# Weighted expert rows added onto the residual rows by indirect DMA, in a streaming encoder step on one Trainium2 core

## The reference

```python
h   = LN0(x) * (1 + scale_m(c)) + shift_m(c)
mix = W_out [ RetentionGroup(h) | StickBreakingGroup(h) ]   # one combined input projection
x   = LN_m(alpha * x + gate_m(c) * mix)                     # x1 below
h   = LN0(x) * (1 + scale_f(c)) + shift_f(c)                # h2 below
x   = LN_f(alpha * x + gate_f(c) * HierMoE(h))
```

## Time and profile before

| what | value |
|---|---|
| median of three runs (lowest, highest) | 1428.81 us (1427.43, 1430.86) |
| the profiled execution's own time | 1431.01 us |
| its span | 1428.9 us |
| PE busy, of the span | 1288.4 us (90%) |
| DVE, ACT, POOL busy | 800.3, 591.2, 335.2 us (56%, 41%, 23%) |
| mean granted clock of TensorE | 0.962 |
| DMA, mean over the span | 164 GB/s |

### The profile page before, as it was taken

One profiled execution on the slowest core, in us unless ns is written; L12 is line 12 of the kernel. 1 busy time (PEld: TensorE's weight loads), 2 busy tenths in 40 slices (PEclk: granted clock), 3 DMA queues, 4 the chain that ended last, 5 costly groups with the idle time before them and its releaser, 6 DMA issues.

```text
span 1428.9 us, 19774 instructions
## 1 busy us (share of the span) xinstructions
PE 1288.4 (90%) x7219; PEld 996.1 (70%) x7220; DVE 800.3 (56%) x1042; ACT 591.2 (41%) x781; POOL 335.2 (23%) x449
## 2 busy tenths in 40 slices
PE   3899999999999989999999988999999999999800
PEld 1665778887787656656687877887777888887700
DVE  5634232324502166666699974557888242558678
ACT  0423022322212267677612232456777253457432
POOL 0032320002200166676346520000000000000073
PEclk9899999999999999999999999999999999999955
DMA  9746110102121261211423378667999161649773
GB/s 337 294 163 196 58 67 1 60 0 75 44 60 42 66 182 31 52 40 31 148 89 104 111 281 352 236 226 278 384 391 389 64 235 59 235 168 381 265 253 121
DMA packets 138776, 234.54 MB, mean 164 GB/s; under 512 B 57328, under 2 KB 58936, under 8 KB 138712
## 3 DMA queue, kind: packets, MB, share of 16 engines
q1 hardware_dynamic: 128440, 196.41, 39.2%
q0 software_dynamic: 6496, 23.60, 4.8%
q10 hardware_dynamic: 3776, 13.67, 2.3%
HBM read 197.96 MB, written 35.68 MB: 164 GB/s over the span
## 4 chain that ended last, share of the span: by engine, by line
PE 63%; issue 12%; DVE 9%; ACT 5%; POOL 5%; DMA 4%; SPq 1%; ACTq 1%; POOLq 0%; DVEq 0%
PE psum L826 58%; POOL arena L2076 3%; PE psum L1051 2%; ACT high L1495 2%; DMA arena<-in_w_ada_ffn 2%; PE psum L1236 1%; DMA arena<-in_w_ada_mix 1%; DVE arena L2015 1%; DVE arena L2014 1%; DVE arena L2007 1%; DVE arena L2005 1%; DVE arena L2006 1%; ACT a_high L1527 1%; PE psum L1242 1%; DMA arena<-h_rows,smalls 1%
## 5 line engine op out<-in xcount | busy, mean ns | idle before, releaser
L826 PE MATMUL psum<-win_high,x_low 128*128 128x512 f32 (+1 forms) x432 | 169.9, 393 | 0.0
L826 PE MATMUL psum<-high,h_high 128*128 128x512 f32 x416 | 164.5, 395 | 2.5 <-DVE h_low L1961 2.5
L826 PE MATMUL psum<-win_high,x_high 128*128 128x512 f32 (+1 forms) x416 | 166.3, 400 | 0.0
L826 PE MATMUL psum<-high,h_low 128*128 128x512 f32 x416 | 162.8, 391 | 0.0
L826 PE MATMUL psum<-win_low,x_high 128*128 128x512 f32 (+1 forms) x416 | 162.8, 391 | 0.0
L826 PE MATMUL psum<-arena 128*64 128x128 f32 (+9 forms) x1324 | 139.4, 368 | 22.1 <-DMA arena<-in_w_ada_mix 17.4
L826 PEld LDWEIGHTS psum<-arena 128*64 128x64 f32 (+6 forms) x1324 | 70.5, 142 | 73.7 <-issue 45.7
L1809 DVE TENSOR_TENSOR_SCAN arena<-arena,psum 128x512 f32<-128x512 f32 (+4 forms) x116 | 109.5, 978 | 19.4 <-ACT arena L1452 19.2
L1956 DVE TENSOR_TENSOR low_odd<-raw_odd,high 128x2048 fp32r<-128x2048 f32 x48 | 107.8, 2288 | 13.7 <-ACT high L1495 13.7
L1956 DVE TENSOR_TENSOR low_even<-raw_even,high 128x2048 fp32r<-128x2048 f32 x48 | 107.7, 2287 | 10.9 <-ACT high L1495 10.8
L2076 POOL TENSOR_TENSOR arena<-arena 128x512 f32<-128x512 f32 (+4 forms) x116 | 108.2, 932 | 9.3
(11 more groups left out here) (264 smaller groups left out, 2475.5 us busy)
## 6 DMA issues: line engine op xcount, KB each, us to landing
raw_even<-in_w_e_gate SPq DMA_DIRECT2D x8, 2048.0 KB, 10.6
raw_even<-in_w_e_up SPq DMA_DIRECT2D x8, 2048.0 KB, 16.5
raw_even<-in_w_e_down SPq DMA_DIRECT2D x8, 2048.0 KB, 14.6
raw_odd<-in_w_e_gate SPq DMA_DIRECT2D x8, 2048.0 KB, 10.4
raw_odd<-in_w_e_up SPq DMA_DIRECT2D x8, 2048.0 KB, 16.7
raw_odd<-in_w_e_down SPq DMA_DIRECT2D x8, 2048.0 KB, 14.8
win<-in_w_in SPq DMA_DIRECT2D x7, 2048.0 KB, 7.9
expert_rows<-arena ACTq DMA_DIRECT2D x26, 512.0 KB, 6.3
```

What stands on the lines that cost most here:

```text
L826: pe_last[0] = nc.tensor.matmul(*x, **y)
```

## The change

- The tensor `expert_rows` is gone. The DRAM tensor of the x1 rows has 128 rows more and that of the h2 rows one more, for slots without a row; SP fills them early with two small DMAs.
- Routing scales w0 and w1 by 1/alpha and splits them into three bf16 parts (six DVE operations on 128x18 or half of that). POOL multiplies the table of slots with each part (three products of 128x594), PE makes 54 small products (128x33) behind the first block's turn, and ACT copies the result, `slot_w`: for every slot its weight, in one column set for prompt rows and another for stream rows. Two more DVE operations make `si`, the row that a slot's result is added to.
- In a block, ACT makes `gate_rows` as the second gate times the slot's weight in place of the copy and the store. DVE adds the first gate times its weight to that (128x1024, from SBUF) and multiplies the down product in PSUM with it into `yb`. These two stand behind pieces 1, 2, 3 of the next weights and ahead of pieces 4, 5. POOL adds `yb` onto the x1 rows in DRAM by an indirect DMA with an add, issued behind the gather for a later block. The product into `yb` waits until the addition before has landed.
- ACT waits for `rows8` ahead of the first block. SP loads expert 1 only when the first gather has landed, and `rows8` behind expert 1. The zero fill is gone.
- In the tail SP loads the nine tiles of summed rows in four groups, once the last addition has landed. DVE takes mean and variance of tiles 0 and 1 by itself; for the others ACT takes the sum and the squares. Then power, norm and store as before.
- In the front `keep_clock` has 15 and 4 products instead of 8 and 5, and 6 new ones stand ahead of the first projection. The first weight chunk is split ahead of the rows, and the four turns of the cached keys of the first pair of heads stand two steps later.

```diff
@@ -375,7 +376,7 @@
-                cache_at[per_pair * pair + 2 + 2 * n] = (pair, n)
+                cache_at[per_pair * pair + 2 + 2 * n + 2 * (pair == 0)] = (pair, n)
@@ -441,8 +442,9 @@
         events.append(("h_turn", 0))
+        split_event("w", 0, 0)
         split_event("x", 0, None)
-        for c in range(KC):
+        for c in range(1, KC):
             split_event("w", 0, c)
@@ -779,18 +787,15 @@
             load_expert(0, 0, (1, 2))
+            sp.wait_ge(s_hg, 16)
             load_expert(1, 1)
-            sp.wait_ge(s_hg, 16)
+            sp.wait_ge(s_ids, 2)
             for slot, src in enumerate((mod_row(1, 0, 2), mod_row(1, 1, 2),
                                         ln_ffn_g[0].unsqueeze(0).to_broadcast([P, D]),
                                         ln_ffn_b[0].unsqueeze(0).to_broadcast([P, D]))):
                 sp.dma_start(rows8[:, slot, :], src).then_inc(s_router, 16)
-            sp.wait_ge(s_zero, 1)
-            total = sp.value_load(table[0:1, 16:17], min_val=1, max_val=MAX_BLOCKS - 1)
-            with sp.Fori(total, MAX_BLOCKS) as b:
-                sp.dma_start(y_dram[bass.ds(b * P, P), :], zero_rows).then_inc(s_fill, 16)
@@ -801,10 +806,11 @@
-            sp.wait_ge(s_edone, EXPERTS - 1)
-            for t in range(TILES):
-                r = rows_of(t)
-                sp.dma_start(x1c[t][0:r], x1_dram[t * P:t * P + r, :]).then_inc(s_x1i, 16)
+            sp.wait_ge(s_summed, 1)
+            for i, tiles in enumerate(SUM_GROUPS):
+                for t in tiles:
+                    r = rows_of(t)
+                    sp.dma_start(ya[t][0:r], x1_dram[t * P:t * P + r, :]).then_inc(s_sum_in[i], 16)
@@ -840,7 +846,7 @@
                     if j >= 2:
-                        keep_clock((8, 5)[j - 2], 4)
+                        keep_clock((15, 4)[j - 2], 4)
@@ -975,6 +981,7 @@
                     if ev[1] == 1:
+                        keep_clock(6, 0)
                         proj(0)
@@ -1217,7 +1224,17 @@
             pe.wait_ge(s_route, 1)
+            pe.wait_ge(s_gi, 2)
             block_turn(0)
+            for s in range(2):
+                tiles = [n for n in range(18) if (n % 9 == LAST) == bool(s)]
+                for part in range(3):
+                    pe.wait_ge(s_bw, part + 1)
+                    for n in tiles:
+                        r = rows_of(n % 9)
+                        last = mm(bank(6)[:, s * MAX_BLOCKS:(s + 1) * MAX_BLOCKS], place_oh[0:r, n, :], block_w[0:r, part, n, :],
+                                  start=(part == 0 and n == tiles[0]), stop=(part == 2 and n == tiles[-1]))
+            last.then_inc(s_ids, 1)
@@ -1236,6 +1253,7 @@
+                        pe.wait_ge(s_gi, 3)
@@ -1505,8 +1523,13 @@
+            act.wait_ge(s_ids, 2)
+            act.wait_ge(s_gi, 2)
+            A(slot_w.rearrange("p s b -> p (s b)"), bank(6)[:, 0:2 * MAX_BLOCKS], ACT.Copy).then_inc(s_gi, 1)
+            act.wait_ge(s_gi, 3)
             act.sem_inc(s_ye, 1)
-            act.sem_inc(s_ys, 16)
+            act.wait_ge(s_ys, 16)
+            act.wait_ge(s_router, 128)
@@ -1531,11 +1554,9 @@
+                        act.wait_ge(s_ye, b + 1)
+                        A(gate_rows, rows8[:, 1], ACT.Copy, scale=slot_w[:, 1, bass.ds(b, 1)]).then_inc(s_gsA, 1)
                         act.wait_ge(s_yp, b + 1)
-                        act.wait_ge(s_ys, 16 * b + 16)
-                        A(yb.rearrange("p (a c) -> p a c", a=2), psum[2][:], ACT.Copy).then_inc(s_ye, 1)
-                        act.wait_ge(s_ye, b + 2)
-                        act.dma_start(y_dram[bass.ds(b * P, P), :], yb).then_inc(s_ys, 16)
...
@@ -1544,15 +1565,17 @@
+                    A(yc[t][0:r], ya[t][0:r], ACT.Copy, accum_out=fin_nm[0:r, t:t + 1]).then_inc(s_crs, 1)
...
@@ -1916,6 +1939,12 @@
             step(TT(w1, w0, dd, ALU.mult))
+            w18 = w01.rearrange("p a t -> p (a t)")
+            step(TS(w18, w18, 1.0 / ALPHA, None, ALU.mult))
+            for part in range(3):
+                step(V.tensor_copy(w_part[part], w18 if part == 0 else w_rest))
+                if part < 2:
+                    step(TT(w_rest, w18 if part == 0 else w_rest, w_part[part], ALU.subtract))
...
@@ -1944,9 +1973,10 @@
+            done(TS(gi, bank(2)[:, 0:MAX_BLOCKS], float(TOK), None, ALU.add), s_gi, 1)
+            step(TS(own_pad, bank(2)[:, 0:MAX_BLOCKS], 0.0, tok_f[:, 0:1], ALU.is_equal, ALU.mult))
+            done(STT(si[:, 1:MAX_BLOCKS + 1], bank(2)[:, 0:MAX_BLOCKS], float(TOK), own_pad, ALU.add, ALU.add), s_gi, 2)
@@ -1987,6 +2017,12 @@
+                        dve.wait_ge(s_gsA, b + 1)
+                        STT(gate_rows, rows8[:, 0], slot_w[:, 0, bass.ds(b, 1)], gate_rows, ALU.mult, ALU.add).then_inc(s_gsD, 1)
+                        dve.wait_ge(s_gsD, b + 1)
+                        dve.wait_ge(s_yp, b + 1)
+                        dve.wait_ge(s_ys, 16 * b + 32)
+                        TT(yb, psum[2].rearrange("p a c -> p (a c)"), gate_rows, ALU.mult).then_inc(s_ye, 1)
@@ -1995,24 +2031,22 @@
-                if t < TILES:
-                    r = rows_of(t)
-                    x = ya[t][0:r]
-                    dve.wait_ge(s_crs, t + 1)
-                    step(STT(x, yc[t][0:r], w1[0:r, t:t + 1], x, ALU.mult, ALU.add))
-                    step(TT(x, x, rows8[0:r, int(t == LAST)], ALU.mult))
-                    done(STT(x, x1c[t][0:r], ALPHA, x, ALU.mult, ALU.add, accum_out=fin_nm[0:r, t:t + 1]), s_cacc, t + 1)
-                    done(TS(fin_nm[0:r, t:t + 1], fin_nm[0:r, t:t + 1], -1.0 / D, None, ALU.mult), s_cve, t + 1)
...
+            for v in range(2):
+                dve.wait_ge(s_sum_in[v], 16 * len(SUM_GROUPS[v]))
+                for hh in range(2):
+                    step(V.bn_stats(stats[:, hh, :], ya[v][:, hh * 512:(hh + 1) * 512]))
+                step(V.bn_aggr(ln_mv[:, v, :], stats.rearrange("p a b -> p (a b)")))
+                step(TS(fin_nm[:, v:v + 1], ln_mv[:, v, 0:1], -1.0, None, ALU.mult))
+                done(TS(fin_sq[:, v:v + 1], ln_mv[:, v, 1:2], EPS / ALPHA ** 2, None, ALU.add), s_fve, v + 1)
+            for v in range(TILES):
+                r = rows_of(v)
+                if v >= 2:
+                    dve.wait_ge(s_csq, v - 1)
+                    done(TS(fin_sq[0:r, v:v + 1], fin_sq[0:r, v:v + 1], 1.0 / D, EPS / ALPHA ** 2, ALU.mult, ALU.add), s_fve, v + 1)
+                dve.wait_ge(s_cnm, v + 1)
+                x = ya[v][0:r]
+                done(STT(x, x, fin_nm[0:r, v:v + 1], rows8[0:r, 2], ALU.add, ALU.mult), s_cg, v + 1)
+                STT(x, x, ln_rstd[0:r, v:v + 1], rows8[0:r, 3], ALU.mult, ALU.add).then_inc(s_cy, 1)
@@ -2124,41 +2157,54 @@
+            pool.wait_ge(s_pad, 32)
+            pool.wait_ge(s_x1o[0], 80)
+            pool.wait_ge(s_x1o[1], 64)
+            pool.wait_ge(s_gi, 1)
+            pool.indirect_dma_start(hg, None, h2_dram, bass.IndirectOffsetOnAxis(ap=gi[:, 0:1], axis=0)).then_inc(s_hg, 16)
+            for part in range(3):
+                w_of_token = w_part[part].unsqueeze(2).to_broadcast([P, 18, MAX_BLOCKS])
+                G.tensor_tensor(block_w[:, part], block_oh, w_of_token, ALU.mult).then_inc(s_bw, 1)
+            pool.wait_ge(s_whg, 16)
             pool.wait_ge(s_gi, 2)
-            pool.indirect_dma_start(hg, None, h2_dram, bass.IndirectOffsetOnAxis(ap=gi[:, 0:1], axis=0)).then_inc(s_hg, 16)
+            pool.indirect_dma_start(x1_dram, bass.IndirectOffsetOnAxis(ap=si[:, 0:1], axis=0), gate_rows, None,
+                                    compute_op=ALU.add).then_inc(s_ys, 16)
+            pool.wait_ge(s_ids, 2)
+            step(G.memset(yb, 0.0))
...
                 pool.sem_inc(s_go, 1)
                 pool.indirect_dma_start(hg, None, h2_dram, bass.IndirectOffsetOnAxis(ap=idc[:, 0:1], axis=0)).then_inc(s_hg, 16)
-            pool.wait_ge(s_fill, 16 * MAX_BLOCKS)
+                pool.wait_ge(s_ys, 16 * b)
+                G.tensor_copy(idc[:, 1:2], si[:, bass.ds(b - 1, 1)]).then_inc(s_idx, 1)
+                pool.wait_ge(s_idx, 2 * b)
+                pool.wait_ge(s_ye, b)
+                pool.sem_inc(s_go, 1)
+                pool.indirect_dma_start(x1_dram, bass.IndirectOffsetOnAxis(ap=idc[:, 1:2], axis=0), yb, None,
+                                        compute_op=ALU.add).then_inc(s_ys, 16)
             pool.wait_ge(s_ys, 16 * total + 16)
+            pool.wait_ge(s_ye, total + 1)
             pool.sem_inc(s_go, 1)
+            pool.indirect_dma_start(x1_dram, bass.IndirectOffsetOnAxis(ap=idc[:, 1:2], axis=0), yb, None,
+                                    compute_op=ALU.add).then_inc(s_ys, 16)
+            pool.wait_ge(s_ys, 16 * total + 32)
             pool.wait_ge(s_edone, EXPERTS)
...
-                    pool.indirect_dma_start(dst[0:r], None, y_dram,
-                                            bass.IndirectOffsetOnAxis(ap=slot_i[0:r, kk, t:t + 1], axis=0)).then_inc(s_y0[t % 4], 16)
...
+            pool.sem_inc(s_summed, 1)
```

(52 more changed lines are left out.)

54 lines of the change are left out of this document (19 added, 35 removed).

## The result

The changed kernel takes 1436.83 us (five runs, 1436.36 to 1438.73) against 1428.81 before: a ratio of 1.006, with an interval from 1.0046 to 1.0075. It is slower by 8.0 us where 7.8 less was forecast, and lies 0.8 above the range. The profiled run's span is 1434.8 against 1428.9.

The account below looks back on a forecast made before the run. PE was taken to bound the experts, with DVE close behind. Front -6.7, cached keys -2.5, first block +8.9, experts +16.6 and tail -24.1 sum to -7.8, so 1421.0 us; range 1408 to 1436.

Parts of the forecast that it names:

- the first block, "+8.9": First expert block: ACT's sigmoid waits for `rows8`, PE's turn falls 7.5 us later, and half-clock products add 1.4.
- The front: Before the router products: clock holds, product 2 takes 1.92, product 3 starts at 39.6, projections run faster; -6.7 us.
- rival (e): Front: the clock falls anyhow, costing 6.2 us, for 1427; chance 0.04.
- The turns of the cached keys: Cached keys: turned two steps later they have landed, so PE's wait of 2.92 goes; -2.5 us, 0.4 left.
- The experts: Nine one-block experts: DVE's two new operations lengthen the cycle to 20.92, +1.84 each; +16.6 us.
- Rival (d): One-block experts: the clock falls in the new waits, 1.4 us in each of nine cycles; +12.6, 1433.6; chance 0.09.
- Rival (b): First block: `rows8` is in time, landing by 879, so no stall; -16.7, 1412; chance 0.17.
- Rival (a): One-block experts: DVE's waits soak up the new work, costing 0.1 a cycle; about 1405; chance 0.11.
- The tail: After the last PE instruction: some 51 us left instead of 75, the addition landing in 5.65; -24.1 us.
- Rival (c): Blocks and tail: the addition lands slowly, DVE's product into `yb` waits for it; 1432 at 17 us; chance 0.07.

Follow-up runs that it names:

- the run without the sum: Changed kernel without DVE's addition of the first gate in `gate_rows` (one operation of 1.28 us in each block); span 1422.2, cycle 19.36.
- the version with the sum made early: Changed kernel with `rows8` loaded first, its wait late, `gate_rows` made behind the sigmoid and summed behind product `a`; 1402.96 us, ratio 0.9805.

## Why the prediction was wrong

**The step that failed is the first block, "+8.9".** Its mechanism was right: ACT waits for `rows8` ahead of its first sigmoid, and PE for ACT. Its size was 19.4 up to the turn and 2.1 behind it (18.68 less 16.57), 12.6 more than forecast: 7.5 by the landing, 3.2 by the path behind it, 1.2 by the gather and 0.7 by the products at half clock (2.1 where 1.4 was taken). The first three:

- The landing. I put 9.7 MB at 409 GB/s between the gather's landing and `rows8`, 25 us in all; it took 32.5 (854.29 to 886.82). The 409 of the earlier trace rows is from a stretch without additions. With them the rate fell to 253 and 279 in parts, as the runs with plain writes (2.65) and with a small first addition (2.1) confirm. The slices from 854 to 886 hold 10.5 MB instead of 9.7, because two additions and two gathers fall into the stretch, where one addition and a gather were counted with some to spare; at 409 this is 2.0. What is left, some 3 us, no run separates. Part of it is the slow start, 152 GB/s from 854 to 858, which the add does not cause: the run with plain writes starts at 139 GB/s (852 to 856).
- The path from there to the turn. I took 1.8 for the sigmoid and two DVE steps. It took 5.0: after the landing 1.8 pass before ACT's next recorded instruction (no run shows what they are; 1.75 to 1.85 pass there in five other runs too), then the function table is loaded, 1.28. I priced the work behind the wait and not what the wait uncovers. Before the change the table was loaded ahead of the gate product at 867.82, and ACT then waited 6.66 for PE (line below, from the timeline before).
- The gather landed 1.2 later than taken, relative to the router products.

```profile
867.28 1.28 ACT L1521 ACT_TABLE_LOAD   x1 [0.85 <-issue]
```

**The front was right in sum for a partly wrong reason.** -8.9 against -9.2. But the clock did not hold through the wait for product 2, as the timeline of the changed kernel shows:

```profile
24.61 6.72 PE L832 MATMUL psum<-smalls 128*128 128x256 f32 x30
33.87 3.57 PE L832 MATMUL psum<-arena 128*32 128x512 f32 x16 [2.54 <-DMA arena<-in_w_ada_mix]
...
40.19 1.92 PE L832 MATMUL psum<-arena 128*32 128x512 f32 x16
```

The 15 products gained nothing at product 2 here (3.57 against 3.64): they start 2 us earlier than I took, because product 1 took 1.92 and not 3.64 in this run, and end 2.5 us before the weights land. That is rival (e). In this run it cost little and not 6.2: product 3 starts at 40.19 where 39.6 was forecast, behind a group that is shorter and runs at full clock. In the run with `rows8` first that group ran at half clock too, and product 3 starts at 42.53. In the run with the front alone the forecast's path came true: PE idles 0.52, product 2 takes 1.92, and product 3 starts at 39.27. The turns of the cached keys, with a first wait of 0.68, for ACT, instead of 2.92 for the keys, and the full clock in the first projections came as forecast.

**The experts were right.** 20.77 for 20.92; nine cycles at 1.69 more are 15.2, and the run without the sum confirms the cause. With the 2.1 behind the stall and the 1.6 below that is 18.9 of the stage's 20.1; no run separates the other 1.2. Rival (d), the clock falling in the new waits, came true in part: in slices of 10 us the granted clock is below 1.00 behind three of the nine waits (0.86, 0.87 and 0.92), and behind two of them PE still had time left in DVE's cycle, so that only the last cost anything, 1.6 us (7.34 less 5.72). Rival (b) did not occur: `rows8` came later than forecast and not earlier. Rival (a) has its answer in the version with the sum made early: DVE's waits can soak up the new work, but only if it stands where the waits are.

**The tail was right**, 50.6 for 51.1. The landing of 6.08 lies in the bounds and near the 5.65 taken. The Trainium skill ("DMA: Bandwidth & Descriptors", section "Rules for kernel authors") says that an accumulate reads its destination and writes it later; the 2.7 us between 3.34 and 6.08 agrees in kind. The estimate of 3.2 from the Trainium skill's fit (same page, section "Anatomy of one DMA — SWDGE (gpsimd) path"), cited in the prediction, meets the plain write (3.34) and not the addition. Rival (c) did not occur: in the trace DVE's 26 products into `yb` wait for PE alone (27.9 us in 11 waits) and never for a landing.

## What to carry to other kernels

A wait costs by where it stands: put it ahead of the instruction that needs the data, not ahead of the loop, and load small things that are needed first ahead of large things that are needed later; here either edit brought 17 us. When pricing a wait, add what it uncovers (here 1.8 before the waiting engine's next instruction, a table load of 1.28, and the half clock of the engine behind it), and take the rate of the queue from a stretch with the same kinds of transfers. On an engine that is nearly full, look for the places where it already waits for others and put new work there: in these runs the same operation cost 1.41 us a cycle between the weights' pieces and nothing behind the product `a`.

## What I had not expected of the hardware

An indirect DMA with an add holds the DMA engines about twice as long as a plain indirect write or a gather of the same size (65.4% against 32.0% and 32.9% of 4 us for 0.52 MB), and leaves less for the plain loads beside it (0.59 MB in 4 us, 1.08 beside the plain write); its own landing, with nothing beside it, is 6.08 (6.04 to 6.40 in all runs with the add) against 3.34 for the plain write.

The same group of products to keep the clock can end in either clock. In the run with the front alone, adaLN product 1 came at half clock, 3.64, and the group of 15 ended close to product 2's weights:

```profile
21.90 3.64 PE L827 MATMUL psum<-arena 128*32 128x512 f32 x16 [1.68 <-DMA arena<-in_w_ada_mix]
...
33.85 1.92 PE L827 MATMUL psum<-arena 128*32 128x512 f32 x16 [0.52 <-DMA arena<-in_w_ada_mix]
```

In the changed kernel product 1 took 1.92, the same group ended earlier, PE idled 2.54 and product 2 came at half clock. All nine runs with the new front fall into these two patterns: in five PE idles 0.52 to 1.22 ahead of product 2, which then takes 1.92, in four 2.42 to 2.69, and it takes 3.10 to 3.57. So the 15 products, meant to end just ahead of the weights, do so only where product 1 comes at or near half clock. What decides that stays open. The clock in the front is part of the spread of the router products: the first projection starts at 49.92 in the run where they come first (823.24) and at 56.21 in the run where they come last (829.57). The runs between do not follow that order, and the rest stays open.
